# A two-block network on one core: side products redistributed, a projection's VectorE and ScalarE work reordered, one norm for two halves of a mixer

## The reference, cut to what matters

```python
mod = cond @ mod_w[layer] + mod_b[layer]          # first block; cond is one vector
h = rmsnorm(x, norm_mix) * (1 + sc1) + sh1
y = hybrid_mixer(h, ...)                          # layer 0
x = x + g1 * y
h = rmsnorm(x, norm_ffn) * (1 + sc2) + sh2
x = x + g2 * peer_ffn(h, ...)                     # the experts; their queries are h @ w_q

# hybrid_mixer: q, k, v of the delta rule go through a causal convolution of width 4
qkv_a = causal_conv_silu(qkv_a, conv_w)
q_a, k_a = l2norm(q_a), l2norm(k_a)
g = -exp(a_log) * softplus(a_a + dt_bias)         # decays, summed within chunks of 64
t_inv = unit_lower_inverse(l_strict)              # by squaring: power @ power, inv @ (eye + power)

# second block, layer 0, over 256 context and 256 latent tokens (512 columns)
# hgrn2: forget-gate heads, chunks of 32, both directions; mlstm: the same with other gates
o = concat([oa, ob])                              # 4 + 4 heads of 128
o = rmsnorm_2(o per head, out_g) * gate           # gate: silu / sigmoid of projections
y = o @ w_out
```

## Time and profile before

| | us |
|---|---|
| median of three runs | 4052.69 |
| the profiled execution's own time | 4046.69 |
| its span, first to last instruction | 4044.7 |
| TensorE, VectorE, ScalarE busy | 3394.5, 2189.0, 1439.6 |
| mean granted TensorE clock | 0.909 of full |

### The profile page before, as it was taken

How to read it: one execution, slowest core, us unless ns; L and a number is a source line. 1 busy time by engine, 2 the same in 40 slices (tenths; PEclk the granted TensorE clock), 3 DMA queues, 4 the chain that set the end, 5 groups by cost and what they waited for, 6 DMA issues and landing times. The chain is left out here.

```text
span 4044.7 us, 55334 instructions
## 1 busy us (share of the span) xinstructions
PE 3394.5 (84%) x20418; PEld 2904.7 (72%) x20418; DVE 2189.0 (54%) x3994; ACT 1439.6 (36%) x2169; POOL 14.4 (0%) x44
## 2 busy tenths in 40 slices
PE   5976799999998577999999994997845999764797
PEld 4844799998887467999988873874623887553697
DVE  3522389876886213898768872245653332224353
ACT  3311344444553223544445542232122322122342
POOL 0000000000000000000000000000000000000000
PEclk7998899999999678999999997998667999987898
DMA  4574466557886314765577861325320332220353
GB/s 155 158 254 136 135 211 201 169 176 221 241 241 200 122 45 133 213 199 168 176 215 241 242 214 48 94 84 210 114 71 27 94 99 89 66 64 0 89 166 121
DMA packets 225073, 596.67 MB, mean 148 GB/s; under 512 B 27424, under 2 KB 97440, under 8 KB 224576
## 3 DMA queue, kind: packets, MB, share of 16 engines
q1 hardware_dynamic: 219504, 588.03, 47.3%
q10 hardware_dynamic: 5328, 5.43, 0.4%
HBM read 558.16 MB, written 35.19 MB: 147 GB/s over the span
## 5 line engine op out<-in xcount | busy, mean ns | idle before, releaser
L1812 PE MATMUL ps<-h_split,split_layer 128*128 128x256 f32 x6144 | 776.4, 286 | 9.5 <-DVE split_layer L1604 9.5
L1812 PEld LDWEIGHTS ps<-h_split,split_layer 128*128 128x128 f32 x6144 | 750.6, 193 | 12.0 <-DVE split_layer L1604 12.0
L1958 PE MATMUL ps<-split_layer,h_split 128*128 128x512 f32 x3072 | 699.8, 390 | 14.0 <-DVE h_split L1942 14.0
L1958 PEld LDWEIGHTS ps<-split_layer,h_split 128*128 128x128 f32 x3072 | 578.7, 188 | 134.6 <-DVE split_layer L1925 14.4
L419 PE MATMUL ps<-h_parts_ffn,split_ffn 128*128 128x512 f32 (+1 forms) x2112 | 376.3, 340 | 34.9 <-DVE split_ffn L394 34.7
L419 PEld LDWEIGHTS ps<-h_parts_ffn,split_ffn 128*128 128x128 f32 x2112 | 330.0, 192 | 81.4 <-issue 37.8
L1604 DVE TENSOR_TENSOR split_layer<-ring,split_layer 128x1024 fp32r<-128x1024 f32 x256 | 311.5, 1219 | 81.1 <-ACT split_layer L1743 79.4
L1925 DVE TENSOR_TENSOR split_layer<-ring,split_layer 128x1024 fp32r<-128x1024 f32 x256 | 313.6, 1225 | 0.1
L394 DVE TENSOR_TENSOR split_ffn<-ring,split_ffn 128x1024 fp32r<-128x1024 f32 x132 | 160.4, 1224 | 265.7 <-ACT split_ffn L384 257.7
L1907 ACT ACTIVATE split_layer<-ring 128x1024 fp32r<-128x1024 f32 x256 | 267.7, 1046 | 4.5 <-PEq L157 4.5
L1743 ACT ACTIVATE split_layer<-ring 128x1024 fp32r<-128x1024 f32 x256 | 268.9, 1051 | 0.7 <-PEq L157 0.7
(11 more groups left out here) (470 smaller groups left out, 3917.4 us busy)
## 6 DMA issues: line engine op xcount, KB each, us to landing
ring<-in_experts SPq DMA_DIRECT2D x512, 512.0 KB, 3.8
ring<-in_mod SPq DMA_DIRECT2D x96, 512.0 KB, 4.9
ring<-in_ada SPq DMA_DIRECT2D x96, 512.0 KB, 4.6
ring<-in_ffn_in SPq DMA_DIRECT2D x88, 512.0 KB, 3.6
hidden_layer<-kept_layer SPq DMA_DIRECT2D x256, 128.0 KB, 2.0
x_sb<-hidden_layer SPq DMA_DIRECT2D x256, 128.0 KB, 3.7
ring<-in_ffn_out SPq DMA_DIRECT2D x44, 512.0 KB, 3.6
ring<-in_peer_q SPq DMA_DIRECT2D x32, 512.0 KB, 3.6
```

The source lines that it names most:

```text
L1812: ins = nc.tensor.matmul(ps[:, 4 + j % 2, 0:T], w[:, part, c], self.hsplit[:, moving, k, :], start=(k == 0 and n == 0), stop=(k == KT - 1 ...
L1958: ins = nc.tensor.matmul(ps[:, 2 * t + h, :], wsplit(j, a)[:, t * P:(t + 1) * P], w[:, b, h * 512:(h + 1) * 512], start=(j == 0 and n == 0 ...
```

## The change

- `hybrid_inputs`: the first three high halves are issued before ScalarE's part for the gates, the fourth behind it; VectorE's part for the gates comes at m=0. The convolutions of the eight q and k tiles are spread (`convolve_at`: ScalarE's part at 5, 6, 8, 9, 11, 12, 14, 15, VectorE's two tiles before). The four value convolutions come behind the 24 tiles. The decays are made at 8, 11, 14 and 15, their exponentials at 16 to 18; the squares' sums at 16, their root at 20.
- `hybrid`: 18 groups of side products and not 20; the block with the addition has four products and not eight. The weights of the last two groups come behind the output projection's. Their products lie in `modulated` (8 and 4) and `split_h` (4), closed by an `end_aside`.
- `mlstm`: no side products in the last two blocks.
- `hgrn_heads`: ScalarE copies `ktok` before the exponentials. Four side products come behind the updates, four behind the state product c = 8.
- The norms of both halves are one function, `gated_norms`. Eight matmuls with a shifted one-hot column gather the eight heads' sums in eight rows of one bank; addition, reciprocal and root run once over these rows; eight matmuls widen them again. Gain and gate are multiplied beforehand. One group of side products lies in its block and the last one in `end_aside`.

```diff
+    def aside_limit(self, n):
+        first = self.products_at
+        return first, min(first + n, 8 * len(self.jobs), first // 8 * 8 + 8 * len(self.aside_banks))
...
+    def aside_products(self, pe, first, last):
+        banks, unit0, moved0 = self.aside_banks, self.aside_unit, self.moved0
+        for i in range(first, last):
+            name, g, c0, n_c = self.jobs[i // 8]
...
+        convolve_at = [5 + m * 3 // 2 for m in range(2 * HEADS)]
+        decays_at = [8, 11, 14, 15]
...
-                    if m == 14:
+                    if m == 16:
                         sums_of_squares()
-                    if m == 21:
+                    if m == 22:
...
+                high(0)
+                high(1)
+                high(2)
+                act.wait_ge(abs_made.sem, up(abs_made))
+                s.activation(beta, beta, ACT.Sigmoid)
+                s.activation(c["decay"], c["a_log"], ACT.Exp)
+                s.activation(tmp, absx, ACT.Exp, scale=-1.0).then_inc(self.act_done.sem, 1)
+                act.wait_ge(self.act_done.sem, self.act_done.up())
+                s.activation(tmp, tmp, ACT.Ln, bias=1.0).then_inc(ln_made.sem, 1)
+                high(3)
+                for m in range(1, N_M + 1):
+                    if 4 <= m < N_M:
                         high(m)
-                    if m:
-                        take(m - 1)
-                    if m == 1:
-
-                        act.wait_ge(abs_made.sem, up(abs_made))
-                        s.activation(beta, beta, ACT.Sigmoid)
-                        s.activation(c["decay"], c["a_log"], ACT.Exp)
-                        s.activation(tmp, absx, ACT.Exp, scale=-1.0).then_inc(self.act_done.sem, 1)
-                        act.wait_ge(self.act_done.sem, self.act_done.up())
-                        s.activation(tmp, tmp, ACT.Ln, bias=1.0).then_inc(ln_made.sem, 1)
-                    if 5 <= m <= 16:
-                        lit(m - 5)
-                    if m == 18:
-
-                        act.wait_ge(inverted.sem, up(inverted))
-                        s.activation(sums, sums, ACT.Sqrt).then_inc(self.rooted.sem, 1)
-                    if m == 19:
+                    take(m - 1)
+                    if m in convolve_at:
+                        lit(convolve_at.index(m))
+                    if m == 16:
                         act.wait_ge(self.exponents_made.sem, up(self.exponents_made))
                         s.activation(rowexp, two(6), ACT.Exp).then_inc(self.exps_made.sem, 1)
                         s.activation(kdec_c, kdec_c, ACT.Exp)
                         s.activation(kbe_c, cum, ACT.Exp)
+                    if m == 17:
+                        s.activation(dec, dec, ACT.Exp, scale=-1.0)
+                    if m == 18:
+                        s.activation(decT, decT, ACT.Exp).then_inc(self.exps_made.sem, 1)
                     if m == 20:
-                        s.activation(dec, dec, ACT.Exp, scale=-1.0)
-                    if m == 21:
-                        s.activation(decT, decT, ACT.Exp).then_inc(self.exps_made.sem, 1)
+                        act.wait_ge(inverted.sem, up(inverted))
+                        s.activation(sums, sums, ACT.Sqrt).then_inc(self.rooted.sem, 1)
+                for m in range(2 * HEADS, 3 * HEADS):
+                    lit(m)
...
-                    if m == 1:
+                    if m == 0:
...
-                    if 3 <= m <= 14:
-                        convolve(m - 3)
+                    if m + 2 in convolve_at:
+                        convolve(convolve_at.index(m + 2))
...
-                    if m == 15:
+                    if m in decays_at:
...
-                    if m == 16:
+                    if m == 18:
...
-                    if m == 19:
+                    if m == 20:
...
-                    if m == 20:
+                    if m == 21:
...
+                for m in range(2 * HEADS, 2 * HEADS + 2):
+                    convolve(m)
...
+                for m in range(2 * HEADS + 2, 3 * HEADS):
+                    convolve(m)
...
-        self.begin_aside([("mod_0", g, 0, 1) for g in range(4, 12)] + [("mod_1", g, 0, 1) for g in range(12)], (7, 6))
+        self.begin_aside([("mod_0", g, 0, 1) for g in range(4, 12)] + [("mod_1", g, 0, 1) for g in range(10)], (7, 6))
...
-                self.aside(block, 8)
+                self.aside(block, 4)
...
+            self.aside(block, 4)
...
+                    if back:
+                        act.wait_ge(turned.sem, turned.n + 1)
+                        s.activation(ktok, ps[:, 1, :], ACT.Copy).then_inc(ktok_done.sem, 1)
                     if front:
                         act.wait_ge(exponents.sem, exponents.n + 1)
                         s.activation(e_inv, e_mid, ACT.Exp, scale=-1.0)
                         s.activation(e_b, b, ACT.Exp)
-                    if back:
-
-                        act.wait_ge(turned.sem, turned.n + 1)
-                        s.activation(ktok, ps[:, 1, :], ACT.Copy).then_inc(ktok_done.sem, 1)
-                    if front:
                         s.activation(dec, ch(b)[:, :, last], ACT.Exp)
...
+                    at0, at1 = self.aside_limit(8)
...
+                        self.aside_products(pe, at0, min(at0 + 4, at1))
                         pe.wait_ge(att_done.sem, att_done.n + 2)
...
-                self.aside(block, 8)
+                            if c == NC // 2:
+                                self.aside_products(pe, min(at0 + 4, at1), at1)
+                    self.aside_counted(block, at0, at1)
+                else:
+                    self.aside(block, 8)
...
-                self.aside(block, 8)
+                self.aside(block, 8 if front else 0)
...
+    def gated_norms(self, o, gates, gain):
+        nc, ps, A = self.nc, self.ps, self.arena
+        v, s = nc.vector, nc.scalar
+        M = 2 * HEADS
+        mark = A.at
+        squares, rows, selector, pick = A.take(M, TA), A.take(TA)[0:M, :], A.take(2 * M - 1), A.take(M, P)[0:M]
+        gate = lambda m: gates[m // HEADS][:, m % HEADS, :]
+        ready, squared, summed, inverted, rooted, widened = (self.a, self.squared, self.summed, self.inverted,
+                                                             self.rooted, self.widened)
+        at0, at1 = self.aside_limit(8)
+        with self.block() as block:
+            @block.scalar
+            def _(act):
+                for m in range(M):
+                    s.activation(squares[:, m, :], o[:, m, :], ACT.Square).then_inc(squared.sem, 1)
+                act.wait_ge(inverted.sem, inverted.n + 1)
+                s.activation(rows, rows, ACT.Sqrt).then_inc(rooted.sem, 1)
+            @block.tensor
+            def _(pe):
+                pe.wait_ge(ready.sem, ready.n + 1)
+                for m in range(M):
+                    pe.wait_ge(squared.sem, squared.n + m + 1)
+                    ins = nc.tensor.matmul(ps[0:M, 0, :], selector[:, M - 1 - m:2 * M - 1 - m], squares[:, m, :],
+                                           start=(m == 0), stop=(m == M - 1))
+                ins.then_inc(summed.sem, 1)
+                self.aside_products(pe, at0, at1)
+                pe.wait_ge(rooted.sem, rooted.n + 1)
+                for m in range(M):
+                    if m >= 6:
+                        pe.wait_ge(self.normalised.sem, self.normalised.n + m - 5)
+                    nc.tensor.matmul(ps[:, 1 + m % 6, :], pick[:, m, :], rows, start=True, stop=True
+                                     ).then_inc(widened.sem, 1)
+            @block.vector
+            def _(dve):
+                v.memset(selector, 0.0).then_inc(self.dve_done.sem, 1)
+                dve.wait_ge(self.dve_done.sem, self.dve_done.up())
+                v.memset(selector[:, M - 1:M], 1.0).then_inc(ready.sem, 1)
+                v.tensor_copy(pick, self.ident[0:M, 0:M].unsqueeze(2).broadcast_to([M, M, P])
+                              ).then_inc(self.dve_done.sem, 1)
+                for m in range(M):
+                    v.scalar_tensor_tensor(gate(m), o[:, m, :], gain[:, m:m + 1], gate(m), ALU.mult, ALU.mult)
+                dve.wait_ge(self.dve_done.sem, self.dve_done.up())
+                dve.wait_ge(summed.sem, summed.n + 1)
+                v.tensor_scalar(rows, ps[0:M, 0, :], 1.0 / P, EPS, ALU.mult, ALU.add).then_inc(self.dve_done.sem, 1)
+                dve.wait_ge(self.dve_done.sem, self.dve_done.up())
+                v.reciprocal(rows, rows).then_inc(inverted.sem, 1)
+                for m in range(M):
+                    dve.wait_ge(widened.sem, widened.n + m + 1)
+                    v.tensor_tensor(o[:, m, :], gate(m), ps[:, 1 + m % 6, :], ALU.mult).then_inc(self.normalised.sem, 1)
+            self.aside_counted(block, at0, at1)
+        ready.up(), squared.up(M), summed.up(), inverted.up(), rooted.up(), widened.up(M), self.normalised.up(M)
+        A.at = mark
...
-        A.at = inner
-        for j, gate in ((0, gate_a), (HEADS, gate_b)):
```

(21 more changed lines are left out.)

51 lines of the change are left out of this document (24 added, 27 removed).

## The result

The changed kernel takes 3984.78 us, the median of four runs (3980.76 to 3987.73), against 4050.65 for the kernel before in the same session (4047.07 to 4061.73). The ratio is 0.9832, its 95% interval 0.9811 to 0.9854: 66 us faster by the medians, against a forecast of 4002. The profiled execution of after took 3987.73 us with a span of 3985.9, the one of before had a span of 4044.7, so the two traces that are compared here differ by 58.8.

The account below looks back on a forecast made before the run. Each block was taken as bounded by its last engine, TensorE being busy 84% overall. Terms -8 - 12.3 + 5.5 - 6.3 - 13 - 15 = -49.1 put the median at 4003.6, stated as 4002; range 3980 to 4028.

Parts of the forecast that it names:

- Part 5: Eight forget-gate blocks: the early copy removes TensorE's wait, -13; the products' new place adds nothing to the sum.
- Part 1: First mixer's projection: TensorE's 4.48 us idle goes, the clock returns for two tiles, spreading gives 1 us: -8.
- Part 2: Block inverse: four products instead of eight leave VectorE's addition last, five blocks of about 2.2 us: -12.3.
- Part 3: Norm before the expert queries: moved products hidden, but a new last block copies, stores and waits: +5.5.
- All under other work: Before the expert queries: products in the norm's, modulation's and split's blocks are hidden, their loads landing in time.
- Part 4: mLSTM's last two blocks lose their side products and shorten by 2.7 and 3.65 us: together -6.3.
- part 6: One norm for both halves after the forget-gate blocks: 36 us to the split instead of 51, -15.
- The bound of -32: Forget-gate blocks: if TensorE can run ahead, VectorE's end bounds each at 13.5 us or less, at most -32 over eight.
- a later stage starting at the lower clock: Example of something outside the forecast's steps changing the time; no size given, chance 0.05.
- the one with the clock up: Rival, recurrent part: removed gaps raise TensorE's clock, forget-gate blocks give -28, norms -19: 3983 us, chance 0.17.
- the slower side: Rival, attention sums and states' matmuls: late loads hold in-order TensorE, +86, 4089 us; chance 0.04, half ending slower.
- The gap in part 1: Rival, first projection: TensorE's gap remains as the gate chain merely moves onto tile 3; -1, 4009 us, chance 0.07.

Follow-up runs that it names:

- d4: Changed kernel with only the gates' edits in the first projection (three high halves ahead, VectorE's part one tile earlier), convolutions and decays in the old order: 3982.1 us.
- a1: Changed kernel with the old side products again: eight in the inverse's addition block, 20 groups in the hybrid mixer, none before the expert queries: 3985.3 us.
- b4: Changed kernel with eight side products again in the mLSTM's last block but one, leaving only copy and store in the norms' closing block: 3978.9 us, ratio 0.9818.
- a3: Changed kernel with all eight products at the forget-gate block's end, the copy of the turned keys still early: 4012.3 us, ratio 0.9898.
- a2: Changed kernel with forget-gate blocks as before: copy behind two exponentials, all eight products at the block's end: 4025.6 us, ratio 0.9938.
- a4: Changed kernel with the copy of the turned keys behind the two exponentials again, products still inside the chain of states: 3997.7 us, ratio 0.9865.

## Why the prediction was right, and where it was not

The direction and the range held (3980 to 4028 with 3984.8 near its lower end); the point, 4002, was 17 too high. That the range held is in part luck: two errors of opposite sign met. Part 5 gave 26.6 more than I took, and a stretch that I had left out lost 10.7; without that loss the time would be near 3974, below the range. By its own steps:

- **Part 1** (-8, measured -5.8): the gap goes and the clock returns at tiles 2 and 3, and both together are worth the 6.9 that was said. Another 1.5 in d4 comes from the tiles behind the sums of squares, which the prediction hadn't named. "I give the spreading 1 us" was wrong in sign: d4 shows a cost of 2.7.
- **Part 2** (-12.3, measured -11.6): right in its stage, block by block 2.4 to 3.0 where 2.2 was said. Together with part 3 it is not seen in the total (a1).
- **Part 3** (+5.5, measured +4.8): right in sum, not in its terms. "All under other work" failed for the products in the modulation's block (a wait for a load of 2.7), and the store's pass was shorter, 3.2 and not 5.5. In the pass that I took as a model four loads stood ahead of two stores; here the last load was issued 2.8 us before the store. That this is the reason is argued from b4, not shown.
- **Part 4** (-6.3, measured -7.5): right. But b4 shows that half of it was no gain: the eight products cost 3.7 in the mLSTM and 7.6 in the closing block of part 6, to which the change moved them.
- **Part 5** (-13, measured -39.6): the mechanism of the wait was right (a3: no wait, blocks of 15.2 to 15.4, 13.3 us in the median). Its two numbers didn't go together: blocks of 15 to 15.5 instead of the 17.5 that the eight took on average are -16 to -20, not -13, and a3's stage, 18.8 shorter than before, shows that. The step that failed is what it said of the products' new place, "They leave TensorE's sum as it is; they help only where TensorE had been paced by VectorE's steps from state to state", and then put at nothing. TensorE had been paced, in every block: L2250's 15 products took 5.6 to 6.4 for 3.6 us of work, and this stood in the timeline. The case was named, as a bound and in a rival, and had no weight in the sum. What a2 to a4 showed in its place is a gain of 18.0 to 23.6 in the seven blocks (27.5 to 27.9 by the medians) from the products alone. The bound of -32 was too narrow as well: it took VectorE's end (2839.75, 13.5 into the block) as fixed, but VectorE's own chain had waited for the updates, and these for the copy that the change moved. 13.5 less the wait of 1.5 and plus 0.9 to the next block is 12.9; the blocks measured 12.4 to 13.3.
- **Part 6** (-15, measured -11.1): the forecast's count of operations was right; the terms mis-sized are the widening, 14.0 and not 9, since the gap in front and the lower clock were not in it, and the closing block, 12.7 and not 11. Between the forecast's own ends, from the last block's end to the split, it is 42.6 and not 36, that is -8.5; another 3 of the 11.1 lie in the ninth forget-gate block, which is shorter too.
- **Not foreseen**: the stretch between inverse and output projection, +10.7 in this pair of profiles. The prediction had 0.05 for "a later stage starting at the lower clock".

Of the rivals, the one with the clock up named this total (3983) with part 5 at its VectorE bound. A higher clock came, 0.84 instead of 0.66, but a3 and a4 show that the order of the work made the gain, edit by edit, and in the changed block VectorE is last, with the same busy time as before. How much of the copy's part came through the clock is open (a3 above). That the total met this rival's number is chance: its part 6 (-19) and its part 5 (-28) both missed. No load came late in the chain: in the seven blocks TensorE has no wait for a load worth a row, so the slower side's mechanism didn't occur. The gap in part 1 did go.

## What to carry to other kernels

An in-order engine that follows another engine step by step has idle time between the steps; independent work belongs there and not at the block's end, and it is worth most of what it took there: 3.4 us a block by the medians, 2.6 to 3.4 by the traces, for products that took 3.6 at the block's end. When a bound is worked out from where another engine ends, take out first the waits that this engine has for the thing that is being moved. And a store that is waited for should not be issued behind loads: it took 6.8 to 8.2 us behind four loads of 512 KB and 3.8 without.
